# Expert rows stored from SyncE's DMA queue instead of ScalarE's

## The reference

```
def hierarchical_moe(h, ...):
    ...
    def expert_block(args):
        xb, e = args
        act = jax.nn.silu(xb @ w_gate[e]) * (xb @ w_up[e])
        return act @ w_down[e]
    ys = lax.map(expert_block, (xs, block_e)).reshape(capacity, d)
    picked = ys[slot].reshape(n, TOP_K, d)
    return jnp.einsum('nkd,nk->nd', picked, weights)
```

## Time and profile before

| | us |
|---|---|
| three runs of the kernel | 2985.43, 2986.63, 2993.77 |
| median | 2986.63 |
| the profiled execution | 2987.3 |
| its span, first to last instruction | 2985.6 |
| first matmul of the expert tiles | 2338.5 |
| end of the last store's packets | about 2964 |

### The profile page before, as it was taken

The page is one execution under the profiler, slowest core; times in us unless marked ns, Lnnn a source line. Parts: engine busy times, 40 slices in busy tenths (PEclk is TensorE's granted clock), DMA queues, the critical chain, the costliest instruction groups (busy, mean ns, idle before and its releaser), DMA issues. The chain is left out here.

```text
span 2985.6 us, 42488 instructions
## 1 busy us (share of the span) xinstructions
PE 2447.6 (82%) x18072; PEld 1899.0 (64%) x18072; DVE 1144.6 (38%) x1421; ACT 810.4 (27%) x995; POOL 10.7 (0%) x56
## 2 busy tenths in 40 slices
PE   5997769977898898699999999959465757877773
PEld 5994559934786765689989989848334423333331
DVE  4752445444534301454554554544422201111111
ACT  3443223231113301444344344344201101111110
POOL 0000000000000000000000000000000000000000
PEclk8998889988877999899999999979786768888887
DMA  4448443465214420454555555334204599888886
GB/s 187 198 169 330 179 170 154 184 275 226 114 59 169 197 84 29 169 185 182 198 184 183 198 185 182 141 135 174 108 0 185 205 384 378 367 359 364 363 360 260
DMA packets 58490, 610.12 MB, mean 204 GB/s; under 512 B 5970, under 2 KB 6354, under 8 KB 13266
## 3 DMA queue, kind: packets, MB, share of 16 engines
q1 hardware_dynamic: 50114, 572.03, 48.3%
q0 software_dynamic: 1872, 23.07, 1.9%
q10 hardware_dynamic: 6336, 12.58, 1.1%
HBM read 674.76 MB, written 14.68 MB: 231 GB/s over the span
## 5 line engine op out<-in xcount | busy, mean ns | idle before, releaser
L1883 DVE TENSOR_TENSOR ffn_w_lo<-ffn_raw,ffn_w_hi 128x2048 fp32r<-128x2048 f32 x128 | 293.1, 2291 | 234.6 <-ACT ffn_w_hi L1876 234.6
L1876 ACT ACTIVATE ffn_w_hi<-ffn_raw 128x2048 fp32r<-128x2048 f32 x128 | 244.9, 1914 | 360.6 <-PE psum L1915 355.8
L1913 PE MATMUL psum<-u_hi,ffn_w_hi 128*128 128x256 f32 x1024 | 291.1, 284 | 15.1 <-DVE ffn_w_lo L1883 14.0
L1914 PE MATMUL psum<-u_lo,ffn_w_hi 128*128 128x256 f32 x1024 | 290.8, 284 | 0.0
L1915 PE MATMUL psum<-u_hi,ffn_w_lo 128*128 128x256 f32 x1024 | 290.8, 284 | 0.0
L2605 PE MATMUL psum<-moe_raw,moe_x_t 128*32 128x512 f32 x1536 | 217.5, 691 | 70.9 <-DMA moe_raw<-in_moe 69.4
L1913 PEld LDWEIGHTS psum<-u_hi,ffn_w_hi 128*128 128x128 f32 x1024 | 197.7, 193 | 16.0 <-DVE ffn_w_lo L1883 14.2
L1913 PE MATMUL psum<-ffn_w_hi,ffn_hid_hi 128*128 128x512 f32 x512 | 199.4, 389 | 0.0
L1914 PE MATMUL psum<-ffn_w_lo,ffn_hid_hi 128*128 128x512 f32 x512 | 199.3, 389 | 0.0
L1915 PE MATMUL psum<-ffn_w_hi,ffn_hid_lo 128*128 128x512 f32 x512 | 199.2, 389 | 0.0
L1914 PEld LDWEIGHTS psum<-u_lo,ffn_w_hi 128*128 128x128 f32 x1024 | 197.7, 193 | 0.5
(11 more groups left out here) (539 smaller groups left out, 4624.4 us busy)
## 6 DMA issues: line engine op xcount, KB each, us to landing
ring<-in_stream SPq DMA_DIRECT2D x107, 2048.0 KB, 10.9
moe_raw<-in_moe SPq DMA_DIRECT2D x96, 2048.0 KB, 18.1
ffn_raw<-in_ffn SPq DMA_DIRECT2D x128, 1024.0 KB, 4.8
moe_raw<-in_moe POOLq DMA_DIRECT2D x48, 2048.0 KB
expert_rows<-moe_stage ACTq DMA_DIRECT2D x48, 256.0 KB
x<-in_x SPq DMA_DIRECT2D x2, 1024.0 KB, 7.9
mem<-in_mem SPq DMA_DIRECT2D x2, 1024.0 KB, 14.6
out<-x SPq DMA_DIRECT2D x2, 1024.0 KB, 4.4
```

Source lines behind the costliest of these rows:

```text
L1876: act.activation(self.w_hi[:, number % self.HIGHS], self.raw[:, number % self.RAWS], ACT.Copy)\
L1883: dve.tensor_tensor(self.w_lo[:, number % self.LOWS], self.raw[:, number % self.RAWS], self.w_hi[:, number % self.HIGHS].bitcast(F32), ALU ...
L1913: pe.matmul(out, lhs[0], rhs[0], start=start, stop=False)
L1914: pe.matmul(out, lhs[0], rhs[1], start=False, stop=False)
```

## The change

The 48 stores move from ACT to SP. ACT's stream loses them, and the `store` helper stands in SP's stream: the store of tile n - 3 is issued behind the loads of tile n (and where tile n is a spare one, for which SP has no loads, by itself), and the last three after the loop. The wait for the take of the tile moves along, from ACT to SP. Nothing is added or left out.

```diff
         @block.sync
         def _(sp):
+            def store(tile):
+                sp.wait_ge(e.y_done, tile + 1)
+                at = ROWS * Sorting.ORDER[tile]
+                rows = io["rows"][at:at + ROWS, :].rearrange("r (q n) -> q r n", q=4)
+                sp.dma_start(rows, e.stage[:, tile % e.STAGED]).then_inc(e.stored[tile % e.STAGED], 16)
             for n in range(3, MOE_TILES):
                 if n % 3 != 1:
                     for u in range(e.UNITS):
                         e.free(sp, n - 2 if n % 3 == 0 else n - 3, u)
                         e.load(sp, n, u)
+                store(n - 3)
+            for tile in range(MOE_TILES - 3, MOE_TILES):
+                store(tile)
...
-            def store(tile):
-                act.wait_ge(e.y_done, tile + 1)
-                at = ROWS * Sorting.ORDER[tile]
-                rows = io["rows"][at:at + ROWS, :].rearrange("r (q n) -> q r n", q=4)
-                act.dma_start(rows, e.stage[:, tile % e.STAGED]).then_inc(e.stored[tile % e.STAGED], 16)
             for g in (0, 2):
                 spread(g)
             for tile in range(MOE_TILES):
...
                 if tile % 2 == 0 and tile + 4 < MOE_TILES:
                     spread(tile + 4)
-                if tile >= 2:
-                    store(tile - 2)
             silu(MOE_TILES - 1)
-            store(MOE_TILES - 2)
-            store(MOE_TILES - 1)
```

## The result

| | before | changed |
|---|---|---|
| median of the runs | 2992.84 us (7 runs, 2985.43 to 2995.64) | 3002.70 us (7 runs, 3001.78 to 3011.94) |
| ratio | | 1.0040, 95% interval 1.0028 to 1.0053 |
| the profiled execution | 2987.3 | 3002.7 |
| first matmul of the expert tiles | 2338.5 | 2339.4 |
| first matmul of tile 9 | 2484.4 | 2487.6 |

The change made the kernel slower: 0.4% by the ratio (some 12 us), 9.9 us by the two medians. The median, 3002.70, lies outside my range (2978 to 3000), and the interval of the ratio leaves out 1. My range was built on a median of 2986.63 from three runs of the kernel before; seven runs of it gave 2992.84. So 6.2 of the 15.7 us between my 2987 and the result belong to that median and not to the change.

A forecast was written before the change was run, and what follows sets the result against it. Four DMA engines carrying both loads and stores were taken as the bound; moved issues and queue order were priced at 0, edges +0.9 on 2987.3, less 0.7 to the median: forecast 2987 us, range 2978 to 3000.

The forecast's parts named there:

- The bound: Expert tiles: the four DMA engines carrying both loads and stores never rest and set the time, 37.3 us a group.
- The chain's long wait for stores: DVE's takes: their 224.4 us of waiting should nearly vanish, with no time won, reappearing as PE waiting for weights.
- Mixing had neither gained nor lost anything: Four engines' queue: load and store packets follow without overlap or pause, so issuing them in order was priced at 0.
- What would show it: Signs of being right: more, shorter share-0.25 windows, takes' waits under 50 us, group 37 us, last store near 2964.
- SP's issue: SP's stream: gains 48 issues of 0.53 us, 25 us in all, free because SP has idle time.
- The edges: First three groups and the end of the expert part: +2.6 - 1.7 = +0.9 us in sum.
- The first gap: At 2372 to 2378: the store of tile 0 now stands behind unit 2 of tile 3, +2.6 us.
- The gaps at 2430 and 2484: Two more stores would fill these gaps, winning 1.4 to 2.4 us, taken as -1.7.
- The end: After the last load: four stores come behind it before and after the change, priced at 0.
- A page and the rows: The skill's rule that another issuing engine changes only sequencer time gives the same 2987; the packet rows side with it.
- rival 1: SP's order starves the loads, 3.0 us a group: 3026 in all 13 groups, 3000 in a third; chance 0.10.
- rival 2: PE becomes the bound at the lower clock; two thirds slow give +59 us, 3046; chance 0.05.

The follow-up runs named there:

- e9: Kernel before, stores still on ACT, each store as four DMAs of 32 rows that can spread over all 16 DMA engines: 2918.2 us, ratio 0.9762.
- e11: Kernel before, stores still on ACT, each store as two DMAs of half the strips, on two engines: 3103.8 us, ratio 1.0395.
- e8: Kernel before, stores still on ACT, with six instead of three buffers for results: ratio 1.0009.
- e12: The changed kernel run again, nothing altered, against the kernel before: ratio 1.0043.
- e13: The changed kernel with six instead of three buffers for results, against the kernel before: ratio 1.0045.
- e1: Kernel before, stores on ACT; only SP's load of unit 1 of each tile 3i+2 is issued late: ratio 1.0003.
- e10: The changed kernel with each store as four DMAs of 32 rows, in SP's queue, against the kernel before: 2910.7 us, ratio 0.9733.
- e2: Kernel before, stores on ACT; SP only waits for the same takes at the same places as in the changed kernel: ratio 1.0007.
- e3: The changed kernel with the spare tiles' stores (every third) issued by ACT again, against the kernel before: ratio 1.0084.
- e6: The changed kernel with stores three in a row once a group and six buffers, against the kernel before: ratio 1.0038.

## Why the prediction was wrong, and where it was right

*The bound: right.* Four engines with loads and stores, 36.87 us of undisturbed packets a group by their records; I had 37.3 from rows and 37.0 from the chain. e9 and e11 settle it.

*The chain's long wait for stores is worth nothing: right.* It fell from 224.4 to 2.3 us and no time was won. PE's wait for weights rose from 69.4 to 145.7; I had forecast about as much as the takes lost, and it was a third of that. e8 shows the same without the move.

*"The work is the same, 37.3 us a group ... Mixing had neither gained nor lost anything ... Priced at 0": **this step failed**.* The packets are the same; their time is not. I had taken one length for load packets, 0.612 us, from a stretch in which all 16 engines were running. After a pause of the twelve many of the first ones take 1 to 2.7 us, and it matters which engines they are on. In the kernel before, the mixing had a use after all: stores piled up, the twelve paused rarely, once in two groups, and each time the four were in stores, whose packets stayed at 84 ns. In the changed kernel the stores are done at once, the pauses are more and shorter, and they fall into the four's loads. The term measured 0.7 to 1.0 us a group from tile 15 to 45 (changed kernel, e12, e13), 8.5 us from tile 9 to 45. That it is the length of the four's load packets is shown by the sums above, since the four never rest in the middle. That the starts of the twelve make them long is shown for a part of it only (below).

*"What would show it" had the sign of it.* I forecast more and shorter windows of share 0.25, three or so a group, and one or two came; I did not ask what each end of such a window costs. The last store was to land within 5 us of 2964 and landed at 2979.7.

*SP's issue: the number was wrong, the conclusion right.* I had 0.53 us an issue; behind two stores the issue of a load lasted 6.8 to 11.9 us. The twelve had to wait for that load, the four had not: in the first such group the twelve start it at 2530.2, and the four come to it at 2537.3, after the loads and stores they still had. e1 paid the same delay and lost nothing.

*The edges: +2.6 - 1.7 = +0.9 predicted, about +2.3 + 3.6 = +5.9 measured.* The first gap is near: the four stood still for 5.9 us there instead of 2.5, +3.4 against the +2.6. The gaps at 2430 and 2484 won nothing: the four stood still for 3.5 us instead of 2.6. The end is not 0, and I put it down to the four having come apart. Their completions of one store lay 0.1 us apart at 2517.6 and 3.4 us at 2931.7 to 2935.1 (in the kernel before 0.7 us at 2956), and the last one decides. No run takes this by itself. Besides, eleven packets of the last stores, from 2971.6 to 2976.8, took 0.1 to 0.9 us each, where no start of the twelve was near.

*A page and the rows.* By the Trainium skill (DMA: Bandwidth & Descriptors, "Issuing engines are not separate DMA queues") another issuing engine changes only the sequencer's time. e9 and e10 bear it out, within 0.4 us of the part. The changed kernel does not: it lost 0.4%, and what moved with the issuer is the order in which packets reach an engine. The measurement decides.

*The chance.* Slower had 0.15, all of it for mechanisms that did not come: e2 excludes rival 1, and against rival 2 stand PE's 145.7 us of waiting for weights and a granted clock of 0.84 over the experts' part in both kernels. One more rival was missing: that a packet's length depends on what the other engines do. And with the kernel before at 2986.63 the same loss of 0.4% would have been 2998.6, inside my range, with the mechanism just as wrong.

What stays open: why the four's loads stretch at some starts of the twelve and not at others (in e12 0.00 at 2643.1, in the changed kernel 1.08 at 2642.2, at the same place of the program); why more runs of stores among the loads make the group longer, which e3 to e6 show (three runs a group +1.3 and +1.5 us, two +0.7 to +1.0, one, or one in two groups, +0.4) but not how; and what pulls the four apart. That more runs of stores are slower holds over these runs, but nothing shows that the starts of the twelve are why. The excess that could be laid to starts of the twelve is 5.5 us in the changed kernel and 2.6 us in e12, of 8.5 and 6.8 lost between tiles 9 and 45; the rest are load packets that are long elsewhere, or on one of the four only.

## What to carry to other kernels

Before a DMA is moved to another queue, count on how many DMA engines it runs (packets beyond the data tell it), and sum packets engine by engine: four DMAs in place of one, each spread over all 16, were worth 2.4 to 2.7% here, and the place of the issue 0.4%, or 0.8% in the worst order tried. Where some engines carry more than others, a tidy order in one queue can be worse than a pile of small stores beside the loads. The longest wait on the chain (224 us here) may be worth nothing; more buffers, which take away that wait and nothing else, tell it in one run.

## What the runs showed of the hardware that I had not expected

- Load packets of 16 KB take 611 ns in steady state and 1 to 2.7 us when many engines start at once; store packets of 2 KB that ran at the same moments stayed at 84 ns.
- In the changed kernel SP was held at the issue of a load for 6.8 to 11.9 us (2517.97 to 2678.90), its semaphore long met, behind two stores of 33 packets on each of four engines. Those stores' own issues took 0.5 us, as ScalarE's did in the kernel before.
- The experts' first matmul came between 2337.2 and 2348.6 us in the sixteen profiles of this study, though the code ahead of it is the same in all kernels. Differences of 10 us between two profiled executions can lie wholly outside the part that was changed; from its own first instruction on, the two profiles of the changed kernel agree to 1.4 us.
